# Moving two of six matmul operands by 64 bytes within a 512-byte period, on one Trainium2 core

## What is computed

```
for i in range(2):
    h = rmsnorm(x, norm1[i])
    mix, xq = mlstm_mixer(h, ...) if i == 0 else diff_attention(h, ...)
    xo = memory_cross_attention(xq, mem, ...)
    x = x + concatenate([mix, xo]) @ w_out[i]
    h = rmsnorm(x, norm2[i])
    gu = h @ w_gate_up[i]
    x = x + (silu(gu[..., :2816]) * gu[..., 2816:]) @ w_down[i]
```

## Time and profile before

| | us |
|---|---|
| median of 3 runs (1203.13 to 1204.05) | 1203.16 |
| the profiled execution, whole time | 1204.02 |
| its span, first to last instruction | 1202.2 |
| TensorE busy in the span | 1196.8 |
| GpSimd busy | 857.4 |
| VectorE busy | 755.9 |
| ScalarE busy | 502.4 |

### The profile page before, as it was taken

The page is one execution under the profiler, slowest core; times in us unless marked ns, Lnnn a source line. Parts: engine busy times, 40 slices in busy tenths (PEclk is TensorE's granted clock), DMA queues, the critical chain, the costliest instruction groups (busy, mean ns, idle before and its releaser), DMA issues.

```text
span 1202.2 us, 18736 instructions
## 1 busy us (share of the span) xinstructions
PE 1196.8 (100%) x6998; PEld 1032.9 (86%) x6998; DVE 755.9 (63%) x1099; ACT 502.4 (42%) x1012; POOL 857.4 (71%) x873
## 2 busy tenths in 40 slices
PE   9999999999999999999999999999999999999998
PEld 7888887788889998899888777778888899889997
DVE  7954434645737991599335888874674599348931
ACT  7522456733203551355231666644431255125510
POOL 7998433566878996699676444445688799669965
PEclk9999999999999999999999999999999999999999
DMA  7234211132223333233433222232232333322332
GB/s 282 92 123 157 71 36 53 53 106 79 92 83 106 106 106 123 88 106 106 126 103 97 80 71 71 64 80 69 71 100 79 118 106 107 105 89 98 115 105 85
DMA packets 35097, 117.43 MB, mean 98 GB/s; under 512 B 4417, under 2 KB 4930, under 8 KB 34886
## 3 DMA queue, kind: packets, MB, share of 16 engines
q1 hardware_dynamic: 33416, 112.83, 29.2%
q10 hardware_dynamic: 1598, 3.51, 1.2%
HBM read 111.07 MB, written 2.11 MB: 94 GB/s over the span
## 4 chain that ended last, share of the span: by engine, by line
PE 97%; DVE 1%; ACT 1%; issue 0%; ACTq 0%; POOL 0%; POOLq 0%
PE PS L1946 69%; PE PS L2284 26%; PE PS L2385 1%; DVE Al L1564 0%; PE PS L2194 0%; PE PS L2413 0%; PE PS L2354 0%; DVE nmB L1850 0%; PE PS L2019 0%; PE PS L2346 0%; PE PS L2338 0%; DVE PB L1862 0%; ACT tmp L1010 0%; ACT tmp L1018 0%; DVE PB L1861 0%
## 5 line engine op out<-in xcount | busy, mean ns | idle before, releaser
L783 POOL TENSOR_TENSOR w_lo<-w_raw,w_hi 128x256 fp32r<-128x256 f32 (+1 forms) x516 | 394.7, 796 | 11.0
L778 POOL TENSOR_SCALAR w_hi<-w_raw 128x1024 fp32r<-128x1024 f32 (+2 forms) x132 | 142.1, 1076 | 283.4 <-PE PS L1946 275.0
L2284 PE MATMUL PS<-tc_hi,w_hi 128*128 128x256 f32 x896 | 250.9, 280 | 0.0
L2284 PE MATMUL PS<-tc_hi,w_lo 128*128 128x256 f32 x896 | 250.0, 279 | 0.0
L2284 PE MATMUL PS<-tc_lo,w_hi 128*128 128x256 f32 x896 | 250.0, 279 | 0.0
L1946 PE MATMUL PS<-Hh,w_hi 128*128 128x512 f32 x560 | 229.3, 410 | 0.0
L1946 PE MATMUL PS<-Hl,w_hi 128*128 128x512 f32 x560 | 219.1, 391 | 0.0
L1946 PE MATMUL PS<-Hh,w_lo 128*128 128x512 f32 x560 | 219.0, 391 | 0.0
L1946 PE MATMUL PS<-Ah,w_hi 128*128 128x512 f32 (+1 forms) x544 | 208.0, 382 | 0.1
L1946 PE MATMUL PS<-Ah,w_lo 128*128 128x512 f32 (+1 forms) x544 | 205.0, 377 | 0.0
L1946 PE MATMUL PS<-Al,w_hi 128*128 128x512 f32 (+1 forms) x544 | 204.9, 377 | 0.0
(11 more groups left out here) (300 smaller groups left out, 1805.5 us busy)
## 6 DMA issues: line engine op xcount, KB each, us to landing
w_raw<-in_wt_dram SPq DMA_DIRECT2D x181, 512.0 KB, 3.6
w_raw<-in_wt_dram SPq DMA_DIRECT2D x16, 384.0 KB, 3.0
w_raw<-in_wt_dram SPq DMA_DIRECT2D x8, 448.0 KB, 3.3
QKR<-QKP ACTq DMA_DIRECT2D x24, 128.0 KB, 4.8
xT<-in_x_t_dram SPq DMA_DIRECT2D x8, 256.0 KB, 4.8
out_dram<-xT SPq DMA_DIRECT2D x8, 256.0 KB, 2.0
mT<-in_mem_t_dram SPq DMA_DIRECT2D x1, 1024.0 KB, 9.5
cn<-in_constants_dram SPq DMA_DIRECT2D x1, 594.5 KB, 6.9
```

The costliest lines, as they stand in the source:

```text
L778: nc.gpsimd.tensor_scalar(w_hi[:, sl, 0:nk], w_raw[:, raw, 0:nk], 0.0, 1.0, ALU.add, ALU.mult).then_inc(w_round, 1)
L783: lo = nc.gpsimd.tensor_tensor(w_lo[:, sl, w], w_raw[:, raw, w], w_hi[:, sl, w].bitcast(F32), ALU.subtract)
L2284: last = nc.tensor.matmul(out_, w[:, b + k], a[:, q, k], start=q < 4 and k == 0 and j == 0, stop=k == 3 and j == 2, skip_group_check=q > 3)
```

## The change

Four tensors that nothing reads or writes are allocated between the buffers. No instruction is added, removed or moved on any engine; only the addresses of operands differ.

```diff
         xT = sb("xT", [P, KD, SEQ])
         Hh = sb("Hh", [P, KD, SEQ], F32R)
+        sb("shift_l", [P, 16])
         Hl = sb("Hl", [P, KD, SEQ], F32R)
+        sb("shift_a", [P, 112])
         Ah = sb("Ah", [P, 8, SEQ], F32R)
+        sb("shift_al", [P, 112])
         Al = sb("Al", [P, 8, SEQ], F32R)
         w_raw = sb("w_raw", [P, RAW, 8, P])
+        sb("shift_w", [P, 16])
         wq_hi = sb("w_hi", [P, 28, P], F32R)
         wq_lo = sb("w_lo", [P, 28, P], F32R)
```

## The result

The changed kernel is slower: 1210.72 us against 1203.61 us (medians of 4 runs each in turn), a ratio of 1.0059 with a 95% interval of 1.0042 to 1.0077, or 7.1 us. The forecast was 1202.1 us with a range up to 1208.5; the sign and the range were missed.

The account below looks back on a forecast made before the run. TensorE's matmul pitches were taken to bound the kernel. For the median, 1203.16 us less 1.0 for `Hl`, with 0 for `Al` and nothing for the rest, gave 1202.1 us; the 8-in-10 range was 1195.5 to 1208.5 us.

Parts of the forecast that it names:

- What bounds the kernel: Whole kernel: TensorE, busy 1196.8 of 1202.2 us, sets the time by its matmuls' pitches; no other engine decides the end.
- the excess beyond the stream: Each matmul's time above streaming its columns: 13.6 ns at 512 columns, 11.1 or 13.3 at 256; all the change can touch.
- The term of `Hl`: 560 matmuls of 512 columns streaming `Hl`, moved plus 64: 1.8 ns less each, 1.0 us less in all.
- the 2.2 ns: Pitch difference at 256 columns: level memory tiles 120.0 ns, `tc` in L2284, 64 above the weights, 117.8 ns.
- The bound of 5.0 us more: Upper bound for `Hl`: 560 matmuls each 9 ns slower, as in the stretch with `wg`; kept as bound, not value.
- the stretch with `wg`: Five intervals, 12.86 to 14.04 us, weights 128 below the streamed operand: 236 ns each, 9 ns above 226.9.
- The term of `Al`: 480 matmuls of 512 columns and 64 of 256 streaming `Al`, moved minus 64: sign unknown, taken as 0.
- The third rival: Down products, output projections, memory tiles: `Al` stream catches up with the weight load, up to 4.9 us more, 1207.1 us; chance 0.20.
- The term of nothing for `Hh` and `Ah`: Matmuls streaming `Hh` and `Ah`, which stay level with the weights: no change counted.
- The terms for `w_raw` and the L2284 matmuls: GpSimd's slack covers `w_raw` 64 below `w_hi`, and the 2688 matmuls of L2284 keep their places: nothing counted for either.
- The rule weighed in the prediction: Every matmul: operands read through two independent ports, so loading next weights costs nothing; addresses cannot matter, sum 0, 1203.2 us.

Follow-up runs that it names:

- e10_everything_up: Kernel before with one 64-byte-per-partition tensor ahead of `Hh`, so all buffers from `Hh` on move by 64 and operand distances stay; 0.9999 of the kernel before.
- e4_all_up: Kernel before with `Hh`, `Hl`, `Ah` and `Al` all moved to 64 bytes above the weights modulo 512; 1.0027 of the kernel before.
- e2_al_down: Kernel before with only `Al` moved, to 64 bytes below `Ah` modulo 512; 1.0025 of the kernel before.
- f1_wlo_up: Kernel before with only the weights `w_lo` moved, to 64 bytes above `w_hi`; 1.0081 of the kernel before, 1212.89 us.
- f4_a_up: Kernel before with only `Ah` and `Al` moved, both to 64 bytes above the weights; 1.0011 of the kernel before.
- e11_tc192: Kernel before with only `tc_hi` and `tc_lo` moved, from 64 to 192 bytes above the weights; 0.9996 of the kernel before.

## Why the prediction was wrong

What bounds the kernel: right. No other engine or wait took part, before or after, and the whole difference is in the pitches. The clock row, read as the top level throughout, hid 3.4 us at 1.2 GHz in the profiled execution. That the excess beyond the stream depends on the operands' places was right as well: `e10_everything_up` against `e4_all_up` shows it.

The term of `Hl` failed, in sign and size. The step was "They come to stand to the weights as `tc_lo` does. I take the 2.2 ns", a difference between matmuls of 256 columns applied to 560 of 512 columns. At 256 columns it was true, as `tc` made level showed (120.0 ns). At 512 level is the best place tried. Instead of 1.0 us less, `Hl` alone cost 5.5 us more in the runs (0.46%), and 5.6 to 6.0 us in the H intervals of its trace against traces at the full clock. The bound of 5.0 us more, from the stretch with `wg`, was about that size, but it was set aside because intervals without `wg` were slow there too. The runs show that this is no objection, since a displaced operand slows its neighbours. Whether the place of `wg` is what makes that stretch slow was not tested. No rival let `Hl` cost time, and the range stopped at 1208.5 us, short of both operands paying, which is what happened.

The term of `Al` was taken as 0 between bounds of 7.4 less and 4.9 more; it was 2.8 us more by its intervals (0.25%, 2.4 us, in the runs of `e2_al_down`). The third rival named this side and place and priced it within its limit. Its mechanism, a stream that overtakes the load started ahead of it, is not shown: 64 above costs more than 64 below for a low part.

The term of nothing for `Hh` and `Ah` failed too. The last sentence of the prediction had this as what would break it, "a displaced stream changes the pitch of its neighbours too". It does: of the 14.4 ns that an H block gained on average (681.5 to 695.9 over blocks that nothing interrupts), each of its three intervals has a share: 4.0, 4.7 and 5.6 ns for those that begin with `Hh`, with `Hl` and again with `Hh`. The excess is no property of one matmul that can be multiplied by a count of 560 or 544.

The terms for `w_raw` and the L2284 matmuls were right: 1.0004 for the one, and 79.14 us against 79.15 for the other.

The rule weighed in the prediction, from the Trainium skill, TensorE: Matmul & The Clock Gate, Part 2, that loading the next weights takes nothing from the running matmul, had been taken to mean that addresses cannot matter. In that sense `f1_wlo_up` contradicts it: only the place of a loaded operand changed, no streamed one, and a block went from 680 to 693 ns. Whether the load takes read bandwidth from the stream, or one load is held up by the one before it, no run tells.

## What to carry to other kernels

When TensorE is full and its fp32r matmuls each load new weights, the places of streamed and loaded operands relative to each other are worth up to 2% here (0.9975 to 1.0173 over the layouts tried), so they should be fixed and measured like any other parameter, and an unrelated buffer put ahead of them can move the time by as much as a small optimisation. A pitch read at one width says nothing of another: level was the best place tried for the 512-column matmuls and the worst on average for the 256-column matmuls of `tc`. Compare blocks of matmuls that repeat, not single ones, since a displaced operand slows its neighbours and the rhythm can also depend on operands that the stretch does not read.

## What the runs showed of the hardware

- The time of a block depends on distances between operands in SBUF that repeat every 256 bytes: at 512 columns 680, 687 and 697 to 703 ns at 0, 64 and 192, and the same at 256, 320 and 448. Moving everything by 64 changed nothing.
- 32 bytes are enough to matter: 700 ns at 32 against 680 at 0 for 512 columns, 350 against 353 at 64 for the 256 columns of `tc`.
- The same instructions at the same distances ran at 113.3 or 117.8 ns each within one execution at a granted clock of 1.00. A wait of 0.2 us changed the pitch in one place (`e4_all_up`, 395.01 us) and not in another (`f4_a_up`, 393.51 us).
- TensorE's granted clock was at its lower level for 3.4 us (793.0 to 796.4 us) in the profiled execution of the kernel before, though TensorE had been busy for 92.48 of the 92.90 us ahead of it. `e11_tc192` has no such stretch at that place.
- Which reads meet, and why level is best at 512 columns, is not settled by these runs.
